# A scaling of attention exponentials placed on GpSimd instead of ScalarE, in a two-layer hybrid encoder

## The reference

```python
# latent heads (8), q and k of width 96, v of width 64
s = einsum('bqhd,bkhd->bhqk', qb, k) * scale
p = softmax(s, axis=-1)
o = einsum('bhqk,bkhd->bqhd', p, v)

# differential heads (4), two maps m of width 64 each, v of width 128
s = einsum('bqhmd,bkhmd->bmhqk', qb, k) * scale + bias
p = softmax(s, axis=-1)
w = p[:, 0] - lam * p[:, 1]
o = einsum('bhqk,bkhd->bqhd', w, v)
```

## Time and profile before

| | us |
|---|---|
| median of 3 runs | 1311.67 (1310.77 to 1313.57) |
| span of the profiled execution, first to last instruction | 1309.4 |
| TensorE busy in that span | 1263.0 (96%) |
| VectorE busy | 836.1 (64%) |
| ScalarE busy | 571.5 (44%) |
| GpSimd busy | 21.3 (2%) |

### The profile page before, as it was taken

One profiled execution on the slowest core, in us unless ns is written; L12 is line 12 of the kernel. 1 busy time (PEld: TensorE's weight loads), 2 busy tenths in 40 slices (PEclk: granted clock), 3 DMA queues, 4 the chain that ended last, 5 costly groups with the idle time before them and its releaser, 6 DMA issues.

```text
span 1309.4 us, 15337 instructions
## 1 busy us (share of the span) xinstructions
PE 1263.0 (96%) x5675; PEld 1011.5 (77%) x5675; DVE 836.1 (64%) x1385; ACT 571.5 (44%) x944; POOL 21.3 (2%) x29
## 2 busy tenths in 40 slices
PE   6999988999999999999999999899999999999997
PEld 5777666778788888888888766677778888888886
DVE  5658878976745554555656688798675555555554
ACT  5236768864322222222333467788442222222223
POOL 0000000000000000000000000000000000000000
PEclk8999898999999999999999999899999999999999
DMA  5331100022433333333314210002223333333321
GB/s 171 107 80 57 33 1 17 33 81 65 124 102 97 95 97 98 97 97 97 97 54 112 57 51 16 17 17 65 80 77 117 97 97 97 97 97 97 97 81 64
DMA packets 142299, 102.39 MB, mean 78 GB/s; under 512 B 5346, under 2 KB 138516, under 8 KB 142228
## 3 DMA queue, kind: packets, MB, share of 16 engines
q1 hardware_dynamic: 142000, 101.40, 26.1%
q10 hardware_dynamic: 100, 0.03, 0.0%
q0 software_dynamic: 128, 0.00, 0.0%
HBM read 99.32 MB, written 2.10 MB: 77 GB/s over the span
## 4 chain that ended last, share of the span: by engine, by line
PE 52%; issue 29%; DVE 10%; ACT 7%; POOL 0%; DMA 0%; POOLq 0%; SPq 0%; DVEq 0%; ACTq 0%
PE bank L1141 47%; DVE pt_lo L833 2%; DVE w_lo L763 2%; PE bank L1223 2%; ACT pt_hi L542 1%; ACT w_hi L500 1%; ACT e_t L523 1%; ACT e_t L533 1%; PE bank L1202 1%; PE bank L1164 1%; DVE k_pack L884 1%; DVE nmx L820 1%; DVE e_t L813 1%; PE bank L1155 1%; PE bank L1317 1%
## 5 line engine op out<-in xcount | busy, mean ns | idle before, releaser
L500 ACT ACTIVATE w_hi<-stage 128x1024 fp32r<-128x1024 f32 (+2 forms) x198 | 196.7, 1000 | 492.4 <-PE bank L1141 451.5
L1141 PE MATMUL bank<-u_hi,w_hi 128*128 128x512 f32 x768 | 305.9, 398 | 6.5 <-DVE u_lo L931 4.8
L1141 PE MATMUL bank<-u_hi,w_lo 128*128 128x512 f32 x768 | 300.0, 391 | 0.0
L1141 PE MATMUL bank<-u_lo,w_hi 128*128 128x512 f32 x768 | 299.9, 390 | 0.0
L763 DVE TENSOR_TENSOR w_lo<-stage,w_hi 128x1024 fp32r<-128x1024 f32 (+2 forms) x192 | 225.0, 1177 | 55.7 <-ACT w_hi L500 55.5
L1141 PE MATMUL bank<-hid_hi,w_hi 128*128 128x512 f32 x512 | 199.2, 389 | 0.0
L1141 PE MATMUL bank<-hid_lo,w_hi 128*128 128x512 f32 x512 | 199.2, 389 | 0.0
L1141 PE MATMUL bank<-hid_hi,w_lo 128*128 128x512 f32 x512 | 199.2, 389 | 0.0
L1141 PEld LDWEIGHTS bank<-u_hi,w_hi 128*128 128x128 f32 x768 | 144.7, 188 | 45.8 <-issue 16.7
L1111 DVE TENSOR_TENSOR h<-h,bank 128x512 f32<-128x512 f32 x128 | 87.7, 687 | 136.1 <-PE bank L1141 136.1
L1141 PEld LDWEIGHTS bank<-u_hi,w_lo 128*128 128x128 f32 x768 | 144.7, 188 | 30.6
(11 more groups left out here) (174 smaller groups left out, 1537.7 us busy)
## 6 DMA issues: line engine op xcount, KB each, us to landing
stage<-in_w_up SPq DMA_DIRECT2D x64, 512.0 KB, 4.0
stage<-in_w_down SPq DMA_DIRECT2D x64, 512.0 KB, 3.5
stage<-in_w_in SPq DMA_DIRECT2D x32, 512.0 KB, 3.9
stage<-in_w_out SPq DMA_DIRECT2D x16, 512.0 KB, 3.4
xin<-in_x SPq DMA_DIRECT2D x4, 512.0 KB, 5.2
stage<-in_w_ukv SPq DMA_DIRECT2D x4, 512.0 KB, 3.2
out<-yout SPq DMA_DIRECT2D x4, 512.0 KB, 3.7
stage<-in_w_uq SPq DMA_DIRECT2D x4, 384.0 KB, 3.2
```

Of the source, the lines that this page charges most:

```text
L500: last = nc.scalar.activation(hi(w_hi, s)[:, :, d:d + n], st(r)[:, :, f:f + n], ACT.Copy)
L1141: mm = nc.tensor.matmul(acc, a, b, start=first and t == 0 and m == 0, stop=last and t == len(terms) - 1 and m == 2)
```

## The change

The two multiplications of a tile of exponentials by one number a row, `t1` (second map of the differential heads) and `normalise` (latent heads), leave ScalarE's queue and are issued on GpSimd, in place, on the same slots, from the same coefficients, with the same semaphores before and after. Instead of an activation with a scale they are a `tensor_scalar` with two multiplications, the second by 1.0. GpSimd now runs through the 48 steps of a layer, and its four `power` calls of the differential heads stand behind the multiplications of n = 8, 12, 16 and 20.

```diff
+            def t1(l, i):
+                pool.wait_ge(coef_ready, val(coef_ready, l, i + 1))
+                t = 2 * (i % 3) + 1
+                nc.gpsimd.tensor_scalar(e_slot(t), e_slot(t), coefs[:, t:t + 1], 1.0, ALU.mult, ALU.mult
+                                        ).then_inc(t1_ready, 1)
+            def normalise(l, i):
+                pool.wait_ge(coef_ready, val(coef_ready, l, DSTEPS + i + 1))
+                t = p_slot(i)
+                nc.gpsimd.tensor_scalar(e_t[:, t, :], e_t[:, t, :], coefs[:, t:t + 1], 1.0, ALU.mult, ALU.mult
+                                        ).then_inc(p_ready, 1)
...
-                for g in range(DIFF_HEADS):
-                    power(l, MISC_AT[f"sub{g}_c"], 3 + g, rs)
+                for n in range(1, STEPS + 1):
+                    if n <= DSTEPS:
+                        t1(l, n - 1)
+                    else:
+                        normalise(l, n - 1 - DSTEPS)
+                    g, r = divmod(n - 8, TT)
+                    if r == 0 and 0 <= g < DIFF_HEADS:
+                        power(l, MISC_AT[f"sub{g}_c"], 3 + g, rs)
...
-            def t1(l, i):
-                act.wait_ge(coef_ready, val(coef_ready, l, i + 1))
-                t = 2 * (i % 3) + 1
-                nc.scalar.activation(e_slot(t), e_slot(t), ACT.Copy, scale=coefs[:, t:t + 1]).then_inc(t1_ready, 1)
-
-            def normalise(l, i):
-
-                act.wait_ge(coef_ready, val(coef_ready, l, DSTEPS + i + 1))
-                t = p_slot(i)
-                nc.scalar.activation(e_t[:, t, :], e_t[:, t, :], ACT.Copy, scale=coefs[:, t:t + 1]
-                                     ).then_inc(p_ready, 1)
...
-                    if 0 < n <= DSTEPS:
-                        t1(l, n - 1)
...
-                    if DSTEPS < n <= STEPS:
-                        normalise(l, n - 1 - DSTEPS)
```

## The result

| | before | after |
|---|---|---|
| median | 1311.36 us (4 runs, 1310.77 to 1313.57) | 1299.90 us (4 runs, 1299.73 to 1300.02) |
| ratio | | 0.9909, 95% interval 0.9897 to 0.9921 |
| span of the profiled execution | 1309.4 us | 1297.9 us |
| TensorE, VectorE, ScalarE, GpSimd busy | 1263.0, 836.1, 571.5, 21.3 us | 1253.6, 834.2, 515.7, 89.3 us |

In this layout the attention of layer 0 now ends at about 284 us instead of 290, that of layer 1 at about 916 instead of 928.

What follows compares the result with a forecast made beforehand. TensorE bounds attention's first window; later it waits on chains ending at ScalarE's queue. Named waits give 3.7 us and short `pt_lo` waits 0.9, so 4.6 a layer, 9.2 for two: 1311.7 - 9.2 = 1302.5 us, range 1293 to 1313.

Steps and rivals of the forecast that it cites:

- What bounds the kernel: Attention: TensorE bounds 92 to 140 us; later it runs short by 3.6 and 8.1 us, where the change can pay.
- From 92 to 140 us TensorE is the bound, whatever ScalarE saves there is covered: First attention window of layer 0: TensorE busy 47.5 of 48 us, so no gain was expected there.
- at nothing: VectorE's waits for the scaled second map, 2.4 and 1.1 us in the first two windows, vanish but add no gain.
- the sum: All counted TensorE waits in attention: 4.6 us per layer, 9.2 us for two, giving 1302.5 us.
- One shift of 0.62 at each place: Each place where TensorE waits gains one scaling's delay of ScalarE's queue, 0.62 us; together 3.7 us, short `pt_lo` waits 0.9.
- `diag` at 0.62: TensorE's wait on `diag`, 1.2 us in layer 0, was to shrink by one shift of 0.62 us.
- GpSimd's duration: One moved scaling of 128x512 on GpSimd: 0.89 us taken, between bounds of 0.53 and 1.18 us.
- The windows of 1.13 and 1.49 us: Time from coefficients or reciprocal to the scaled tile's reader, differential and tightest latent steps; 0.89 us fits, costing 0.
- The slow rival: GpSimd's scalings outlast their windows, eating the gain at 1.56 us; 1324.3 us at d = 2.0; above 1314, chance 0.13.
- cost 0: GpSimd's power calls for differential heads, queued behind multiplications, were to start as before and cost 0.
- The port rival: VectorE instructions with two SBUF inputs stand until GpSimd's scaling ends; decides from 1.16 us; 1308 to 1315 us, chance 0.04.
- The clock rival: Shorter waits spare one low-clock stretch a layer, 6.9 us more, 1295.6 us; range 1289 to 1298, chance 0.10.

## Why the prediction was right, and where it was not

- **What bounds the kernel, and that ScalarE's queue is what the change removes:** right for the latent steps, and shown by the run that gives the queue its length back. In the differential steps 2.1 of 5.0 us stay in that run, where VectorE's wait for the scaled map is short as well.
- **"From 92 to 140 us TensorE is the bound, whatever ScalarE saves there is covered":** wrong by 1.8 us in layer 0 and about as much in layer 1. It was read from a busy time of 47.5 of 48 us, in which pauses of 0.1 to 0.3 us do not show. The cause is what the prediction put aside "at nothing", VectorE's wait for the scaled map. Before:

```profile
120.99 0.75 DVE L813 SCALAR_TENSOR_TENSOR e_t<-e_t,coefs 128x512 f32<-128x512 f32 x1 [0.91 <-ACT e_t L517]
...
125.05 0.68 DVE L799 CUSTOM_DVE_ANT_0 e_t<-bank,consts 128x512 f32<-128x512 f32 x1
...
125.80 0.50 PE L1141 MATMUL bank<-dk_hi,dq_hi 64*128 64x512 f32 x1 [0.24 <-DVE nmx L799]
```

  After, in VectorE's timeline, the same L817 starts at 119.00 with no wait and the same `ttr` at 123.26, 1.8 us earlier; TensorE's scores follow without a pause. The first windows of the two layers are 3.5 us that the sum did not have.
- **"One shift of 0.62 at each place":** half right. At the two `k_pack` places of the latent steps ScalarE's chain is gone altogether, 0.90 and 0.96 us, where 0.62 was given; the third, 0.5 us at a differential step, `v_pack` (1.6) and the long wait before a turn (2.3) gave nothing, where 0.62 each was taken. No scaling was last on the chain of these two. Ahead of the turn ScalarE makes five copies in a row. Ahead of `v_pack` the exponential starts when VectorE's row maximum is done, 0.04 us behind it, with the scaling in front of it and without (before, then after):

```profile
182.48 0.69 DVE L820 TENSOR_REDUCE nmx<-bank 128x1 f32<-128x512 f32 x1
183.21 0.69 ACT L533 ACTIVATE e_t<-bank,nmx 128x512 f32<-128x512 f32 x1
...
181.06 0.69 ACT L541 ACTIVATE e_t<-bank,nmx 128x512 f32<-128x512 f32 x1 [0.59 <-DVE nmx L824]
```

  The short `pt_lo` waits gave most of their visible size and the hidden 0.16 us besides: turns and values at 214, 280, 286 and 289 us are 1.66 us, where 0.9 was taken.
- **`diag` at 0.62:** wrong in sign. TensorE's waits on it are 1.6 instead of 1.2 us, and the `diag` behind the long power call delays the scores at 164.1 us (1.62 instead of 0.21 us in the table).
- **GpSimd's duration:** 0.697 us, between the bounds of 0.53 and 1.18 and under the 0.89 taken; it changed no term, since both fit the window.
- **The windows of 1.13 and 1.49 us:** right, by the runs with more passes and with one multiplication. The slow rival's price was 9 steps a layer; 0.52 a step at 1.57 us cost 5.7 us by 182 us and 4.8 us from 290 to 816 us against the change: 9 to 11 steps. Its point of decision, 1.56 us, was within what the measurement can tell.
- **The power calls "cost 0":** wrong. The port rival was priced for scalings, and there it has no case: no VectorE instruction with two SBUF inputs ran beside one in the changed kernel. It came at the one power call where ScalarE's earlier copy had let VectorE's low part move in front, and there GpSimd is the one that is held, a direction that the rival did not price. With one more pass on GpSimd it does come at the scalings too: the low part of `q_pack` starts at 185.58 us, 0.27 before the pass ends, and takes 0.80 instead of 0.68 us.
- **The clock rival:** half of it came with the forecast, one stretch of 3.4 us at half clock less in each layer, 3.4 us in all where 6.9 was priced.
- **The sum:** 9.2 us predicted, 11.5 measured. That the size came near is in part luck, by three errors: the first windows give 3.5 us that were not counted and the clock about 3.4 that was not in the sum. The remaining 4.6 us, half of the 9.2, are what the counted places give, less what is lost at `diag` and at the scores of 164 us.
- **What would show it:** of VectorE's waits for the scaled map (3.5 us in layer 0) one of 0.8 us is left, and the L523 line gone: right. "`k_pack` about a third of before": 0.5 us of 2.0, right. "`pt_lo` for `pt_hi` cut by about half": wrong, 12.7 us from 182 to 290 us, where it was 14.5; VectorE waits on, but TensorE no longer waits behind it. "ScalarE near 111 us": 117.95 us for the same work, 27.9 less than before, which is 0.58 a scaling. Busy time counts overlapping activations once, so the shift of 0.62 and not the duration of 0.718 should have been subtracted. "L799 unchanged": wrong, 3.1 us where it was 2.4. "Its place taken by `pt_lo` and about 0.6 us shorter": the place, but not shorter. "VectorE's unchanged": right, 161.1 us and 161.9 before.

What stays open: how the 16.2 us of the second extra pass divide between waits, held scalings and clock, and why leaving out one multiplication more than doubles the instruction's time. The low clock's places were not steered by any run; that they move with the waits is seen, what makes a stretch begin is not.

## What to carry to other kernels

Take a multiplication off an in-order queue when the waits of the bounding engine lead back to that queue, even if they name another engine, and put it where the time from its last input to its reader is longer than it takes: here 1.13 us for 0.70 on an engine that was 2% busy. Look for small waits in distances between starts, not in busy shares: 0.16 us of every pause of TensorE, and a whole window's 1.8 us, were inside "busy". Once an engine holds something with a short deadline, what stands in front of it eats its slack: 1.42 us of diagonals made VectorE wait 1.17 us for the scaling behind them. And look at what the other engine starts meanwhile: 2.4 us subtractions on GpSimd gained 3.9 us beside the latent steps, where they met few VectorE instructions with two inputs in SBUF, and lost 4.7 once they stood beside the differential ones too, where they held `weights` and low parts for up to 2.2 us.

## What the runs showed of the hardware that was not expected

- GpSimd multiplies a 128x512 float32 tile by a column and by 1.0 in 697 ns, by two constants in 618 ns, by a column alone in 1567 ns; a 128x128 one by a column and 1.0 in 374 to 390 ns (VectorE 282). A subtraction of two 128x1024 SBUF tiles takes it 2397 ns, VectorE 1219.
- A 4-column power call of 1.01 us takes 1.51 when a VectorE instruction with two SBUF inputs has started 0.05 us ahead of it, and 1.02 when that starts 0.08 us behind it. The VectorE instruction keeps 0.68 us in both.
- A VectorE instruction with two SBUF inputs that starts while a GpSimd subtraction or scaling runs can be held, for a little less than what the other had to go: 1.83 us of 2.03, 0.50 of 0.63, 0.12 of 0.27. The power call that starts second shows the same: 0.50 us of 0.63, 0.38 of 0.52.
- Not every pair does this. Behind a power call (0.08, 0.36 and 0.55 us behind its start), and behind the 1567 ns form of the scaling with 0.43 us to go, VectorE keeps its 0.68 to 0.69 us. Why these differ no run here shows.
